# A hybrid mLSTM and gMLP step: rounding and subtraction of the state C placed ahead of each weight split, and small work of a head moved from VectorE to ScalarE

## The chip, the cores and the metric

The kernel runs on one core of one Trainium2 chip. The time is the device time of that core in microseconds. Three runs of the kernel before took 1510.98, 1510.55 and 1510.87 us, a median of 1510.87 us. All five engines run their own instruction streams and wait for each other by semaphores: TensorE (PE; PEld is its weight load), VectorE (DVE), ScalarE (ACT), GpSimd (POOL) and SyncE (SP), which issues most of the transfers.

## The reference

One layer over a prompt of 256 tokens and a batch of 8 sequences with 4 new tokens each, so 288 columns in all. Everything is fp32.

```python
h = RMSNorm_pre(x);  P = h @ w_in          # 2048 x 20496 columns: q k v o za, gates, u vb zb, ga gb
qk = silu(causal_conv4(cat(q, k)))         # depthwise, 4 taps, history from state_conv_qk
# mLSTM, 8 heads of 256, per chunk of tokens:
s    = (q . k) * wts
num  = s @ v + sc_inter * (C @ q)          # C: the old state of the head, [value x key]
den  = sum(s) + sc_inter * (n . q)
C_new = decay * C + sum ws * v k^T;  n_new = decay * n + sum ws * k
y_a = sigmoid(o) * headnorm(num / max(|den|, exp(-m))) * silu(za)
y_b = u * (tril(W_s) @ LN(vb) + b) * silu(zb)          # gMLP branch
merged = sigmoid(ga) * (y_a @ w_pa) + sigmoid(gb) * (y_b @ w_pb)
y = x + RMSNorm_post(merged @ w_out)
```

The prompt starts from a zero state. The eight sequences each have their own C and n for every head, and both are read for `C @ q` and `n . q` and written back updated.

## The kernel before, in words

**Weights.** All weights are streamed as 104 pairs of 256 columns. A pair is four chunks of 512 rows. For each chunk SyncE loads `raw[:, c]`, ScalarE rounds it to fp32r (`split_hi`, L811, `whi`), and VectorE subtracts to get the rest (`split_lo`, L1088, `wlo`). TensorE then makes 24 products of 288 columns (`chunk`, L439 to L441: hi by hi, hi by lo, lo by hi). Each of `raw`, `whi` and `wlo` has one place per chunk number, so `split_hi` of a pair's chunk c waits until TensorE has finished chunk c of the pair before. A split is therefore made nearly a whole pair ahead of its use, and each chunk on TensorE sets free the next split on ScalarE and VectorE.

**Stages.** vb pairs, u and zb pairs (gMLP), the first half of the merge, then the loop over eight heads, then the second half of the merge and the output projection. The change touches the loop over heads alone.

**A head** has five pairs on TensorE: q, k, v, o, za. The small work of the head stands between the chunks, in an order written out by hand on each engine:

- While TensorE is on the k pair, VectorE and ScalarE split the v pair. ScalarE copies q's results into a padded tile (`to_padded`, L910 and L913), VectorE makes the convolution (`conv`, L1359 and L1363; four taps by two halves of 312 columns, into `acc`, which is `hb` in the trace), and ScalarE applies Silu (L919, L921). The same is done for k one pair later.
- The old state C of sequence b is used by `inter(h, b)` on TensorE (L602 and L604, four products of about 256 columns). It stands after v chunks 1, 2, 3 (b = 0, 1, 2), o chunks 0 to 3 (b = 3 to 6) and za chunk 0 (b = 7). What it needs is made in three steps: `turn_blocks` (VectorE, L1384) transposes 32 by 32 blocks of C into `Yb`, which has two places; `ct_copy` (ScalarE, L930) rounds it to `CTh`, of which there is one, so it waits until inter(b - 1) is finished; `ct_split` (VectorE) puts n's two columns beside `CTh` (L1374) and subtracts to get `CTl` (L1375).
- After o chunk 0 TensorE makes q . k (L654), for which it needs `kv4`, a copy of k made by VectorE (L1472). After o chunk 3 it turns k and v of the sequences (L671, L672), for which it needs `ktok` from ScalarE (L972, L974) and the second part of `kv4` (VectorE, L1492). ScalarE copies these out as `kst`, `vst` and two more tiles (L978 to L982) and signals `kvs_ev`; VectorE corrects `kst` and `vst` (L1509, L1511) and signals `st_lo`.
- After za chunk 0 TensorE turns v (L685). It waits for `st_lo`, since the result goes to PSUM bank 5, from which `kst` and `vst` are read. Then come two `new_state` (L615, two products each), which need the masked values `vm` of sequence b (`of_sequence`, VectorE, L1390, four places). Six more follow by za chunk 3. VectorE adds each to the old state (`add_state`, L1397).

In the lists below a chunk's pair is the one that TensorE works on or the one that is split; the text says which.

Of the kernel before, what the change touches and what calls it, by code (L numbers as in the profile page):

```python
# [26 lines left out]
F32 = mybir.dt.float32  # L27
F32R = mybir.dt.float32r
ALU = mybir.AluOpType
# [63 lines left out]
def build(nc, x_prompt, x_sample, state_C, state_n, state_m, state_conv, g_pre, w_in, b_ig, b_fg,  # L93
# [258 lines left out]
    def of_c(b):  # L352
        return Yb[:, b % 2]
# [451 lines left out]
    def _(act):  # L805
        def split_hi(pair, c, first=False):

            act.wait_ge(raw_landed[c], 16 * pair + 16)
            if not first:
                act.wait_ge(chunk_done, 4 * pair - 3 + c)  # L810
            nc.scalar.activation(whi[:, c], raw[:, c], ACT.Copy).then_inc(hi_ready, 1)  # L811
# [106 lines left out]
        def silu(j, done):  # L918
            nc.scalar.activation(qk[:, j:j + 2, 0:TP], acc[:, :, 0:TP], ACT.Silu).then_inc(done, 1)  # L919
            for jj in range(2):  # L920
# [2 lines left out]
                    acc[:, jj, XPS:XPW].rearrange("p (b t) -> p b t", t=HIST + TS)[:, :, 0:TS],  # L923
                    ACT.Silu).then_inc(done, 1)

        def ct_copy(h, b):
            act.wait_ge(block_turned, 8 * h + b + 1)
            if b > 0:
                act.wait_ge(inter_mm, 8 * h + b)
            nc.scalar.activation(CTh[:, :, 0:DH], of_c(b), ACT.Copy).then_inc(ct_ev, 1)  # L930

        with act.Fori(0, HEADS) as h:
# [7 lines left out]
            to_padded(0, 0, q_ev)  # L940
            act.wait_ge(q_ev, 3 * h + 3)
            act.sem_inc(slot_free[0], 1)

            for c in range(CHUNKS):
                split_hi(H0 + 2 + 5 * h, c)
# [6 lines left out]
            to_padded(2, 1, k_ev)  # L952
            act.wait_ge(k_ev, 3 * h + 3)
            act.sem_inc(slot_free[1], 1)

            for c in range(CHUNKS):
                split_hi(H0 + 3 + 5 * h, c)
                ct_copy(h, c)
                if c == 2:
                    act.wait_ge(conv_step, 16 * h + 16)  # L960
                    silu(2, silu_k)
# [2 lines left out]
            act.sem_inc(slot_free[0], 1)  # L964

            for c in range(CHUNKS):
                split_hi(H0 + 4 + 5 * h, c)
                ct_copy(h, 4 + c)
                if c == 2:

                    act.wait_ge(kt_t, h + 1)
                    nc.scalar.activation(ktok[:, 0, :], ps[:, 5, 0:DH], ACT.Identity,  # L972
                                         scale=gq[:, 0, ds(h + 64, 1)])
                    nc.scalar.activation(ktok[:, 1, :], ps[:, 5, DH:2 * DH], ACT.Identity,  # L974
                                         scale=gq[:, 1, ds(h + 64, 1)]).then_inc(kt_ev, 1)
                if c == 3:
                    act.wait_ge(kvs_t, h + 1)
                    nc.scalar.activation(kst[:], ps[:, 5, 0:DH], ACT.Identity, scale=gq[:, 2, ds(h + 64, 1)])  # L978
                    nc.scalar.activation(vst[:], ps[:, 5, DH:2 * DH], ACT.Copy)
                    nc.scalar.activation(ktok[0:S, 2, :], ps[0:S, 5, 0:DH], ACT.Identity,  # L980
                                         scale=gq[0:S, 2, ds(h + 64, 1)])
                    nc.scalar.activation(vtok_h[0:S, 2, 0:DH], ps[0:S, 5, DH:2 * DH],  # L982
                                         ACT.Copy).then_inc(kvs_ev, 1)
            act.wait_ge(nn_ev, h + 1)
            nc.scalar.activation(og[:], results(1), ACT.Tanh, scale=0.5).then_inc(slot_free[1], 1)

            for c in range(CHUNKS):
                split_hi(H0 + 5 + 5 * h, c)
                if c == 0:
                    act.wait_ge(vt_t, h + 1)  # L990
                    nc.scalar.activation(vtok_h[:, 0:2, 0:DH], ps[:, 5, :].rearrange("p (t v) -> p t v", t=2),
                                         ACT.Copy).then_inc(vt_ev, 1)
                    act.wait_ge(inter_mm, 8 * h + 8)
                    nc.scalar.activation(vtok_h[S:2 * S, 2, :], ps[S:2 * S, 4, 0:DH + 2],
                                         ACT.Copy).then_inc(lo_rows, 1)
# [88 lines left out]
    def _(dve):  # L1084
# [267 lines left out]
        def conv(h, j, blk, taps):  # L1352

            for tap in taps:
                for jj in range(2):
                    w_at = par0[:, ds(2 * h + (32 * tap + blk + jj), 1)]
                    out, src = acc[:, jj, 0:CW], xp[:, j + jj, tap:tap + CW]
                    if tap == 0:
                        ins = nc.vector.tensor_scalar(out, src, w_at, par1[:, ds(2 * h + (blk + jj), 1)],  # L1359
                                                      ALU.mult, ALU.add)  # L1360
                    else:
                        dve.wait_ge(conv_step, 16 * h + (4 * j + 2 * tap + jj - 1))
                        ins = nc.vector.scalar_tensor_tensor(out, src, w_at, out, ALU.mult, ALU.add)  # L1363
                    ins.then_inc(conv_step, 1)

        def own(part_):

# [3 lines left out]
        def ct_split(h, b):  # L1371

            dve.wait_ge(ct_ev, 8 * h + b + 1)
            nc.vector.tensor_copy(CTh[:, :, DH:DH + 2], nT[:, :, ds(h + 8 * b, 1), :].squeeze(2).bitcast(F32))  # L1374
            nc.vector.tensor_tensor(CTl[:, b % 2], of_c(b), CTh[:, :, 0:DH].bitcast(F32),  # L1375
                                    ALU.subtract).then_inc(ct_lo, 1)

        def turn_blocks(h, b):
# [3 lines left out]
            if b >= 2:  # L1382
                dve.wait_ge(inter_mm, 8 * h + b - 1)
            nc.vector.transpose(of_c(b).rearrange("p k (j s) -> p j k s", s=32),  # L1384
                                Xb[:, b]).then_inc(block_turned, 1)

        def of_sequence(h, b):
            if b >= 4:
                dve.wait_ge(cs_mm, 8 * h + b - 3)
            nc.vector.tensor_scalar(vm[:, b % 4, :], vst[:].bitcast(F32), mask8[:, b:b + 1], None,  # L1390
                                    ALU.mult).then_inc(vm_set, 1)

        def add_state(h, b):
            if b % 4 == 0:
# [6 lines left out]
        with dve.Fori(0, HEADS) as h:  # L1401
# [27 lines left out]
            for c in range(CHUNKS):  # L1429
                split_lo(H0 + 2 + 5 * h, c)  # L1430
                if c == 0:
                    dve.wait_ge(q_ev, 3 * h + 3)
                    dve.wait_ge(hist_set, h + 1)
                    conv(h, 0, 0, (0, 1))
                if c == 1:
                    conv(h, 0, 0, (2, 3))
                if c == 3:
                    dve.wait_ge(silu_q, 3 * h + 3)
                    qs = Steps(dve, q_step, 2 * h)
# [5 lines left out]
                    qs(nc.vector.tensor_copy(own(0), scaled))  # L1445
                    last = nc.vector.tensor_tensor(own(S), scaled, own(0).bitcast(F32), ALU.subtract)
                    last.then_inc(qm_set, 1)
                    turn_blocks(h, 0)

            for c in range(CHUNKS):  # L1450
                split_lo(H0 + 3 + 5 * h, c)
                ct_split(h, c)
                turn_blocks(h, c + 1)
                if c == 0:
                    dve.wait_ge(k_ev, 3 * h + 3)
                    conv(h, 2, 16, (0, 1))
                if c == 1:
                    conv(h, 2, 16, (2, 3))
                if c == 2:
# [10 lines left out]
                if c == 3:  # L1470
                    dve.wait_ge(silu_k, 3 * h + 3)
                    nc.vector.tensor_copy(kv4[:, 0].rearrange("p j (n s) -> p j n s", s=S),  # L1472
                                          bc(qk[:, 2:4, TP:T], 2, [P, 2, P // S, S])).then_inc(kv4_set, 1)

                    dve.wait_ge(wsb_set, h + 1)
                    for j in range(2):
                        nc.vector.scalar_tensor_tensor(
# [6 lines left out]
                                               mybir.AxisListType.X, ALU.add))  # L1484
                    of_head = nacc[:, :, 0:NB, ds(h, 1)].squeeze(3)
                    nc.vector.tensor_tensor(of_head, of_head, added, ALU.add).then_inc(nn_ev, 1)

            for c in range(CHUNKS):
                split_lo(H0 + 4 + 5 * h, c)
                if c == 2:  # L1490
                    dve.wait_ge(v_ev, h + 1)
                    nc.vector.tensor_copy(kv4[:, 1].rearrange("p j (n s) -> p j n s", s=S),  # L1492
                                          bc(vz[:, :, TP:T], 2, [P, 2, P // S, S])).then_inc(kv4_set, 1)
                ct_split(h, 4 + c)
                if c < 3:
                    turn_blocks(h, 5 + c)
                if c == 0:
                    dve.wait_ge(s_mm, h + 1)
                    dve.wait_ge(w_exp, h + 1)
                    nc.vector.scalar_tensor_tensor(W[:, 0:384], ps[:, 5, 0:384], DH ** -0.5, W[:, 0:384],  # L1500
                                                   ALU.mult, ALU.mult)
                    nc.vector.tensor_copy(W[S:2 * S, 384:416], ident[S:2 * S, S:2 * S])
                    nc.vector.scalar_tensor_tensor(W[0:S, 384:416], ps[0:S, 5, 384:416], DH ** -0.5,
                                                   W[0:S, 384:416], ALU.mult, ALU.mult).then_inc(p_set, 1)
                if c == 3:

                    dve.wait_ge(kvs_ev, h + 1)
                    for rows in (slice(S, 2 * S), slice(3 * S, P)):
# [1 line left out]
                                                       kst[rows].bitcast(F32), ALU.mult, ALU.subtract)  # L1510
                    nc.vector.tensor_tensor(vst[2 * S:P], ps[2 * S:P, 5, DH:2 * DH], vst[2 * S:P].bitcast(F32),  # L1511
                                            ALU.subtract).then_inc(st_lo, 1)
                    dve.wait_ge(st_lo, h + 1)
                    for b in range(4):
                        of_sequence(h, b)

            for c in range(CHUNKS):
                split_lo(H0 + 5 + 5 * h, c)
                if c == 0:
                    add_state(h, 0)  # L1520
                    of_sequence(h, 4)
                    add_state(h, 1)
                    of_sequence(h, 5)
                if c == 1:

                    dve.wait_ge(num_mm, h + 1)
# [6 lines left out]
                    den(nc.vector.tensor_tensor(q3[:], q3[:], gq[:, :, ds(h + 32, 1)].squeeze(2), ALU.max))  # L1533
                    nc.vector.reciprocal(r3[:], q3[:]).then_inc(r_set, 1)
                    add_state(h, 2)
                    of_sequence(h, 6)
                    dve.wait_ge(sq_set, 3 * h + 3)
                    nc.vector.tensor_scalar(stat[:], q3[:], 1.0 / DH, EPS, ALU.mult, ALU.add).then_inc(var_set, 1)
                    add_state(h, 3)
                    of_sequence(h, 7)  # L1540
                    dve.wait_ge(rs_set, h + 1)
                    nc.vector.tensor_tensor(f3[:], r3[:], rstd[:], ALU.mult).then_inc(f_set, 1)
                if c == 2:
# [299 lines left out]
```

## Time and profile before

| | |
|---|---|
| median of three runs | 1510.87 us |
| the profiled execution | 1510.56 us |
| its span, first to last instruction | 1509.1 us |
| TensorE busy | 1486.6 us |
| VectorE busy | 935.5 us |
| ScalarE busy | 664.4 us |
| GpSimd busy | 184.5 us |
| granted TensorE clock, mean | 0.997 |
| one head, TensorE's distance from inter(0) to the next head's | about 79.1 us |

The profile is of one execution. Busy time counts an engine's instructions from start to end; on TensorE neighbours overlap, so a matmul of 288 columns lasts 0.29 us in the rows while the next starts 0.13 us after it. What matters is then the distance from one start to the next. In a row of the timeline a bracket gives the idle time before the instruction and what ended it.

### The profile page before, as it was taken

What the parts mean: (1) busy time and instruction counts of PE and PEld (TensorE: products, weight loads), DVE (VectorE), ACT (ScalarE), POOL (GpSimd) and SP (SyncE); (2) the same over time, 40 slices, a digit from 0 to 9 for tenths busy, and PEclk for the clock granted to TensorE, in tenths of its full rate; (3) what the DMA queues carried; (4) which work ended last, traced back from release to release, by engine and by line L of the source; (5) the groups of instructions that cost most, each with busy time, mean ns of one, the idle gap of its engine ahead of it and who ended that gap; (6) DMA issues with size and microseconds to landing.
All of it is one profiled execution on the core that took longest, in us unless ns stands there. A gap on an engine that the chain in (4) does not pass through costs nothing. (4 is left out here: it accounts for less than half of the span.)

```text
span 1509.1 us, 31633 instructions
## 1 busy us (share of the span) xinstructions
PE 1486.6 (99%) x11131; PEld 1472.1 (98%) x11131; DVE 935.5 (62%) x1617; ACT 664.4 (44%) x949; POOL 184.5 (12%) x331
## 2 busy tenths in 40 slices
PE   9999999999999999999999999999999999999996
PEld 9999999999999999999999999999999999999996
DVE  7756565554444458787777777786868554544444
ACT  6433433433333335454545555545455433333442
POOL 4000000001000002213030303031312000000000
PEclk9999999999999999999999999999999999999998
DMA  7765555557556577696959595959697556565543
GB/s 233 208 163 147 175 151 173 157 165 223 181 175 182 175 206 175 187 254 163 278 152 288 145 292 146 284 152 281 158 274 173 197 175 182 169 183 192 172 154 140
DMA packets 310006, 289.62 MB, mean 192 GB/s; under 512 B 82728, under 2 KB 297456, under 8 KB 309168
## 3 DMA queue, kind: packets, MB, share of 16 engines
q1 hardware_dynamic: 291424, 243.05, 57.7%
q0 software_dynamic: 18288, 45.97, 8.9%
q8 instruction: 24, 0.39, 0.1%
q14 instruction: 14, 0.11, 0.0%
q10 hardware_dynamic: 256, 0.10, 0.0%
HBM read 263.62 MB, written 25.42 MB: 192 GB/s over the span
## 5 line engine op out<-in xcount | busy, mean ns | idle before, releaser
L1088 DVE TENSOR_TENSOR wlo<-raw,whi 128x1024 fp32r<-128x1024 f32 x416 | 507.2, 1222 | 494.9 <-ACT whi L811 494.0
L439 PE MATMUL ps<-xh,whi 128*128 128x288 f32 x2560 | 760.5, 297 | 0.0
L441 PE MATMUL ps<-xh,wlo 128*128 128x288 f32 x2560 | 755.2, 295 | 0.0
L440 PE MATMUL ps<-xl,whi 128*128 128x288 f32 x2560 | 754.1, 295 | 0.0
L811 ACT ACTIVATE whi<-raw 128x1024 fp32r<-128x1024 f32 x416 | 440.5, 1060 | 711.9 <-PE ps L441 691.2
L439 PEld LDWEIGHTS ps<-xh,whi 128*128 128x128 f32 x2560 | 481.0, 188 | 0.3
L441 PEld LDWEIGHTS ps<-xh,wlo 128*128 128x128 f32 x2560 | 480.6, 188 | 0.0
L440 PEld LDWEIGHTS ps<-xl,whi 128*128 128x128 f32 x2560 | 480.3, 188 | 0.2
L440 PE MATMUL ps<-yl,whi 128*128 128x288 f32 x512 | 151.6, 296 | 0.0
L441 PE MATMUL ps<-yh,wlo 128*128 128x288 f32 x512 | 150.9, 295 | 0.0
L439 PE MATMUL ps<-yh,whi 128*128 128x288 f32 x512 | 150.1, 293 | 0.0
L439 PEld LDWEIGHTS ps<-yh,whi 128*128 128x128 f32 x512 | 96.3, 188 | 0.0
L440 PEld LDWEIGHTS ps<-yl,whi 128*128 128x128 f32 x512 | 96.2, 188 | 0.0
L441 PEld LDWEIGHTS ps<-yh,wlo 128*128 128x128 f32 x512 | 96.2, 188 | 0.0
L440 PE MATMUL ps<-ml,whi 128*128 128x288 f32 x248 | 73.4, 296 | 0.0
L439 PE MATMUL ps<-mh,whi 128*128 128x288 f32 x248 | 73.4, 296 | 0.0
L441 PE MATMUL ps<-mh,wlo 128*128 128x288 f32 x248 | 73.1, 295 | 0.0
L1769 POOL DMA_DIRECT2D out_dram<-cst x64 | 35.9, 562 | 244.4 <-DVE cst L1468 238.9
L930 ACT ACTIVATE CTh<-Yb 128x512 fp32r<-128x512 f32 x64 | 40.2, 628 | 20.3 <-PE ps L604 14.0
L439 PEld LDWEIGHTS ps<-mh,whi 128*128 128x128 f32 x248 | 46.7, 188 | 0.0
L440 PEld LDWEIGHTS ps<-ml,whi 128*128 128x128 f32 x248 | 46.6, 188 | 0.0
L441 PEld LDWEIGHTS ps<-mh,wlo 128*128 128x128 f32 x248 | 46.6, 188 | 0.0
(361 smaller groups left out, 1289.5 us busy)
## 6 DMA issues: line engine op xcount, KB each, us to landing
raw<-in_w_in_dram SPq DMA_DIRECT2D x320, 512.0 KB, 3.9
raw<-in_w_pb_dram SPq DMA_DIRECT2D x32, 512.0 KB, 3.6
Cin<-in_state_mlstm_C_dram POOLq DMA_DIRECT2D x16, 1024.0 KB, 8.7
Xb<-in_state_mlstm_C_dram SPq DMA_DIRECT2D x256, 64.0 KB, 3.8
out_dram<-Cin POOLq DMA_DIRECT2D x16, 1024.0 KB, 6.3
raw<-in_w_pa_dram SPq DMA_DIRECT2D x32, 512.0 KB, 3.5
raw<-in_w_out_dram SPq DMA_DIRECT2D x32, 512.0 KB, 3.6
part_d<-part POOLq DMA_DIRECT2D x8, 288.0 KB, 3.2
```

What stands on the lines that cost most here:

```text
L439: nc.tensor.matmul(out, whi[:, c, kk, cols], mh_[:, k, :], start=(k == 0), stop=False)
L440: nc.tensor.matmul(out, whi[:, c, kk, cols], ml_[:, k, :], start=False, stop=False)
L441: last = nc.tensor.matmul(out, wlo[:, c, kk, cols], mh_[:, k, :], start=False, stop=(k == KT - 1))
L811: nc.scalar.activation(whi[:, c], raw[:, c], ACT.Copy).then_inc(hi_ready, 1)
L930: nc.scalar.activation(CTh[:, :, 0:DH], of_c(b), ACT.Copy).then_inc(ct_ev, 1)
L1088: nc.vector.tensor_tensor(wlo[:, c], raw[:, c], whi[:, c].bitcast(F32), ALU.subtract).then_inc(lo_ready, 1)
L1769: pool.dma_start(blocks_of(conv_p_v, h, s, g), cst[g:g + 3, 2 * s:2 * s + 2, :]).then_inc(cst_out, 16)
```

## The change

Five edits, all in the loop over heads.

1. On ScalarE `ct_copy` stands ahead of `split_hi` in each step of the k-side and v-side loops; on VectorE `ct_split` and the next `turn_blocks` stand ahead of `split_lo`. Before, each split came first.
2. n's two columns of `CTh` are written by ScalarE in `ct_copy` and no longer by VectorE in `ct_split`.
3. The first tap of the convolution (`first_tap`) is an Identity activation with scale and bias on ScalarE, right after q's and k's results are copied.
4. The masked values `vm` (`of_sequence`) are made by ScalarE: four after `og`'s Tanh and ahead of the next split, two and two after the splits of chunks 1 and 2.
5. On VectorE `turn_blocks` of b = 0 and 1 both stand after the v pair's split 2. The sums for n (L1477 to L1486) move from the end of one loop to after the za pair's split 1, and the products of `W` (`p_set`) and the second `kv4` come after `ct_split`, `turn_blocks` and `split_lo` of their step.

```diff
+        def first_tap(h, j, blk):
+            for jj in range(2):
+                nc.scalar.activation(acc[:, jj, 0:CW], xp[:, j + jj, 0:CW], ACT.Identity,
+                                     bias=par1[:, ds(2 * h + (blk + jj), 1)],
+                                     scale=par0[:, ds(2 * h + (blk + jj), 1)]).then_inc(conv_step, 1)
+
+        def of_sequence(h, b):
+            if b >= 4:
+                act.wait_ge(cs_mm, 8 * h + b - 3)
+            nc.scalar.activation(vm[:, b % 4, :], vst[:].bitcast(F32), ACT.Identity,
+                                 scale=mask8[:, b:b + 1]).then_inc(vm_set, 1)
+
         def ct_copy(h, b):
             act.wait_ge(block_turned, 8 * h + b + 1)
             if b > 0:
                 act.wait_ge(inter_mm, 8 * h + b)
+            nc.scalar.activation(CTh[:, :, DH:DH + 2], nT[:, :, ds(h + 8 * b, 1), :].squeeze(2).bitcast(F32), ACT.Copy)
             nc.scalar.activation(CTh[:, :, 0:DH], of_c(b), ACT.Copy).then_inc(ct_ev, 1)
...
             act.sem_inc(slot_free[0], 1)
+            act.wait_ge(hist_set, h + 1)
+            first_tap(h, 0, 0)
...
-
-            for c in range(CHUNKS):
+            first_tap(h, 2, 16)
+
+            for c in range(CHUNKS):
+                ct_copy(h, c)
                 split_hi(H0 + 3 + 5 * h, c)
-                ct_copy(h, c)
...
             for c in range(CHUNKS):
+                ct_copy(h, 4 + c)
                 split_hi(H0 + 4 + 5 * h, c)
-                ct_copy(h, 4 + c)
...
             nc.scalar.activation(og[:], results(1), ACT.Tanh, scale=0.5).then_inc(slot_free[1], 1)
+            act.wait_ge(st_lo, h + 1)
+            for b in range(4):
+                of_sequence(h, b)
 
             for c in range(CHUNKS):
                 split_hi(H0 + 5 + 5 * h, c)
+                if c == 1:
+                    of_sequence(h, 4)
+                    of_sequence(h, 5)
+                if c == 2:
+                    of_sequence(h, 6)
+                    of_sequence(h, 7)
...
             dve.wait_ge(ct_ev, 8 * h + b + 1)
-            nc.vector.tensor_copy(CTh[:, :, DH:DH + 2], nT[:, :, ds(h + 8 * b, 1), :].squeeze(2).bitcast(F32))
...
-                    conv(h, 0, 0, (0, 1))
+                    conv(h, 0, 0, (1,))
                 if c == 1:
                     conv(h, 0, 0, (2, 3))
+                if c == 2:
+                    turn_blocks(h, 0)
+                    turn_blocks(h, 1)
...
-                    turn_blocks(h, 0)
-
-            for c in range(CHUNKS):
+
+            for c in range(CHUNKS):
+                ct_split(h, c)
+                if c > 0:
+                    turn_blocks(h, c + 1)
                 split_lo(H0 + 3 + 5 * h, c)
-                ct_split(h, c)
-                turn_blocks(h, c + 1)
                 if c == 0:
                     dve.wait_ge(k_ev, 3 * h + 3)
-                    conv(h, 2, 16, (0, 1))
+                    conv(h, 2, 16, (1,))
...
+            for c in range(CHUNKS):
+                ct_split(h, 4 + c)
+                if c < 3:
+                    turn_blocks(h, 5 + c)
+                split_lo(H0 + 4 + 5 * h, c)
+                if c == 2:
+                    dve.wait_ge(v_ev, h + 1)
+                    nc.vector.tensor_copy(kv4[:, 1].rearrange("p j (n s) -> p j n s", s=S),
+                                          bc(vz[:, :, TP:T], 2, [P, 2, P // S, S])).then_inc(kv4_set, 1)
```

**Where ScalarE's order moves.** The engine is ScalarE, at the end of the steps that split the za pair, when TensorE has finished o chunk 3. `whi<-raw` is `split_hi` of za chunk 3, `CTh<-Yb` is `ct_copy` of b = 7, `kst`, `vst`, `ktok`, `vtok_h` are the copies that end in `kvs_ev`, and `og` is the Tanh. Before:

```order
L811 ACTIVATE whi<-raw 128x1024 [waits chunk_done,raw_landed3]
L927 REGISTER_ALU
L930 ACTIVATE CTh<-Yb 128x2x256 [waits inter_mm,block_turned]
L978 ISA [waits kvs_t]
L978 ACTIVATE kst<-ps,gq 128x256
L979 ACTIVATE vst<-ps 128x256
L980 ACTIVATE ktok<-ps,gq 32x256
L982 ACTIVATE vtok_h<-ps 32x256
L985 ACTIVATE og<-ps 128x576 [waits nn_ev]
```

After:

```order
L939 REGISTER_ALU
L942 ISA [waits inter_mm,block_turned]
L942 ACTIVATE CTh<-nT 128x2x2
L943 ACTIVATE CTh<-Yb 128x2x256
L811 ACTIVATE whi<-raw 128x1024 [waits chunk_done,raw_landed3]
L994 ISA [waits kvs_t]
L994 ACTIVATE kst<-ps,gq 128x256
L995 ACTIVATE vst<-ps 128x256
L996 ACTIVATE ktok<-ps,gq 32x256
L998 ACTIVATE vtok_h<-ps 32x256
L1001 ACTIVATE og<-ps 128x576 [waits nn_ev]
L935 ACTIVATE vm<-vst,mask_56 128x256 [waits st_lo]
```

The copy of C now stands ahead of the split, and both still stand ahead of `kst`; the split now lies between the wait for `inter_mm` and `kst`. Behind `og` there is a wait for `st_lo` and four copies to `vm`.

**Where VectorE's order moves, I.** The engine is VectorE, one step earlier (split of za chunk 2, TensorE on o chunk 3). `kv_134<-vz` is the second part of `kv4`, for which TensorE's L671 waits; `CTl` is `ct_split`, `Yb<-Xb` is `turn_blocks`. Before:

```order
L1087 REGISTER_ALU
L1088 TENSOR_TENSOR wlo<-raw,whi 128x1024 [waits hi_ready]
L1492 COPY kv_134<-vz 128x256 [waits v_ev]
L1373 REGISTER_ALU
L1374 ISA [waits ct_ev]
L1374 COPY CTh<-nT 128x2x2
L1375 TENSOR_TENSOR CTl<-Yb,CTh 128x512
L1384 STREAM_TRANSPOSE Yb<-Xb 128x8x2x32 [waits inter_mm]
```

After:

```order
L1393 REGISTER_ALU
L1394 TENSOR_TENSOR CTl<-Yb,CTh 128x512 [waits ct_ev]
L1403 STREAM_TRANSPOSE Yb<-Xb 128x8x2x32 [waits inter_mm]
L1112 REGISTER_ALU
L1113 TENSOR_TENSOR wlo<-raw,whi 128x1024 [waits hi_ready]
L1498 COPY kv_134<-vz 128x256 [waits v_ev]
```

The copy to `kv4` stood behind the split alone; now `ct_split` (with its wait for `ct_ev`) and `turn_blocks` stand ahead of the split too.

**Where VectorE's order moves, II.** The engine is VectorE, at the start of the steps that split the o pair (TensorE on v chunks 1 and 2). `qm` is the last work on q. Before:

```order
L1446 TENSOR_TENSOR qm<-qp,qm 128x2x8x4 [waits q_step]
L1381 REGISTER_ALU
L1384 STREAM_TRANSPOSE Yb<-Xb 128x8x2x32 [waits block_in0]
L1087 ISA
L1088 TENSOR_TENSOR wlo<-raw,whi 128x1024 [waits hi_ready]
L1373 ISA
L1374 REGISTER_ALU [waits ct_ev]
L1374 COPY CTh<-nT 128x2x2
L1375 TENSOR_TENSOR CTl<-Yb,CTh 128x512
L1384 STREAM_TRANSPOSE Yb<-Xb 128x8x2x32
L1359 ISA [waits k_ev]
```

After:

```order
L1462 TENSOR_TENSOR qm<-qp,qm 128x2x8x4 [waits q_step]
L1393 ISA
L1394 TENSOR_TENSOR CTl<-Yb,CTh 128x512 [waits ct_ev]
L1112 ISA
L1113 TENSOR_TENSOR wlo<-raw,whi 128x1024 [waits hi_ready]
L1383 REGISTER_ALU [waits k_ev]
L1384 ISA [waits conv_step]
L1384 SCALAR_TENSOR_TENSOR hb<-xp,par_58,hb 128x312
```

The transposition of b = 0 is gone from this place (it stands a step earlier), `ct_split` of b = 0 stands ahead of the split, the transposition of b = 1 is gone too, and of the convolution only the second tap is left here.

## Rows read from the trace of the kernel before

**Rows 1.** The page: busy time of each engine.

```profile
PE 1486.6 (99%) x11131; PEld 1472.1 (98%) x11131; DVE 935.5 (62%) x1617; ACT 664.4 (44%) x949; POOL 184.5 (12%) x331
```

**Rows 2.** Who waited for whom, TensorE weight loads: us in total, times, longest.

```profile
PEld ps L602 <- DVE CTl L1375: 12.7, 24, 1.1
...
PEld ps L685 <- issue: 2.3, 8, 0.3
...
PEld ps L654 <- DVE kv L1472: 1.9, 8, 0.2
```

**Rows 3.** Timeline of TensorE, third head: start us, us, what, count.

```profile
741.75 0.29 PE L441 MATMUL ps<-xh,wlo 128*128 128x288 f32 x1
...
742.97 0.28 PE L604 MATMUL ps<-CTl,qm 128*128 128x256 f32 x1
...
743.09 0.29 PE L439 MATMUL ps<-xh,whi 128*128 128x288 f32 x1
...
754.66 0.48 PE L654 MATMUL ps<-qk 128*128 128x256 f32 x1
```

**Rows 4.** Timeline of VectorE, third head, the same stretch.

```profile
739.96 0.70 DVE L1384 STREAM_TRANSPOSE Yb<-Xb 128x512 f32<-128x512 f32 x1
...
740.59 1.19 DVE L1088 TENSOR_TENSOR wlo<-raw,whi 128x1024 fp32r<-128x1024 f32 x1
...
741.76 0.68 DVE L1375 TENSOR_TENSOR CTl<-Yb,CTh 128x512 fp32r<-128x512 f32 x1
...
742.37 0.70 DVE L1384 STREAM_TRANSPOSE Yb<-Xb 128x512 f32<-128x512 f32 x1
...
744.57 1.22 DVE L1088 TENSOR_TENSOR wlo<-raw,whi 128x1024 fp32r<-128x1024 f32 x1
...
754.36 0.25 DVE L1472 COPY kv<-qk 128x256 f32<-128x256 f32 x1
```

**Rows 5.** Timeline of ScalarE, third head, the same stretch.

```profile
737.21 0.28 ACT L913 ACTIVATE xp<-ps 128x32 f32<-128x32 f32 x2
...
738.89 1.06 ACT L811 ACTIVATE whi<-raw 128x1024 fp32r<-128x1024 f32 x1 [1.40 <-PE ps L441]
...
743.34 0.63 ACT L930 ACTIVATE CTh<-Yb 128x512 fp32r<-128x512 f32 x1 [0.20 <-PE ps L604]
```

**Rows 6.** Third head, last chunk of the o pair: timelines of TensorE, then VectorE.

```profile
764.77 0.29 PE L439 MATMUL ps<-xh,whi 128*128 128x288 f32 x1
...
767.96 0.27 PE L671 MATMUL ps<-ident,kv 128*128 128x128 f32 x1
...
765.15 1.23 DVE L1088 TENSOR_TENSOR wlo<-raw,whi 128x1024 fp32r<-128x1024 f32 x1 [1.15 <-ACT whi L811]
...
766.29 0.29 DVE L1492 COPY kv<-vz 128x256 f32<-128x256 f32 x1
```

**Rows 7.** Third head, last o chunk to new states: ScalarE, VectorE, TensorE.

```profile
768.22 1.06 ACT L811 ACTIVATE whi<-raw 128x1024 fp32r<-128x1024 f32 x1 [1.82 <-PE ps L441]
...
769.19 0.62 ACT L930 ACTIVATE CTh<-Yb 128x512 fp32r<-128x512 f32 x1
...
769.71 0.46 ACT L978 ACTIVATE kst<-ps,gq 128x256 fp32r<-128x256 f32 x1
...
770.06 0.37 ACT L979 ACTIVATE vst<-ps 128x256 fp32r<-128x256 f32 x1
...
771.25 0.99 DVE L1509 SCALAR_TENSOR_TENSOR kst<-ps,gq,kst 32x256 fp32r<-32x256 f32 x2
...
772.71 1.15 DVE L1390 TENSOR_SCALAR vm<-vst,mask 128x256 fp32r<-128x256 f32 x4
...
768.75 0.29 PE L604 MATMUL ps<-CTl,qm 128*128 128x256 f32 x1
...
772.82 0.63 PE L685 MATMUL ps<-ident,vz 128*128 128x128 f32 x4
...
773.21 0.72 PE L615 MATMUL ps<-kst,vm 128*128 128x256 f32 x4
```

More of the change, by code:

```diff
@@ L1357, in conv @@
                     out, src = acc[:, jj, 0:CW], xp[:, j + jj, tap:tap + CW]
[L1358 to L1364, printed above, removed]
+                    dve.wait_ge(conv_step, 16 * h + (4 * j + 2 * tap + jj - 1))
+                    nc.vector.scalar_tensor_tensor(out, src, w_at, out, ALU.mult, ALU.add).then_inc(conv_step, 1)
         def own(part_):
@@ L1385, in turn_blocks @@
                                 Xb[:, b]).then_inc(block_turned, 1)
[L1387 to L1391, printed above, removed]
         def add_state(h, b):
@@ L1473, in _ @@
                                           bc(qk[:, 2:4, TP:T], 2, [P, 2, P // S, S])).then_inc(kv4_set, 1)
+            for c in range(CHUNKS):
[7 more added lines that the diff above has]
+                                          bc(vz[:, :, TP:T], 2, [P, 2, P // S, S])).then_inc(kv4_set, 1)
+                if c == 0:
+                    dve.wait_ge(s_mm, h + 1)
+                    dve.wait_ge(w_exp, h + 1)
+                    nc.vector.scalar_tensor_tensor(W[:, 0:384], ps[:, 5, 0:384], DH ** -0.5, W[:, 0:384],
+                                                   ALU.mult, ALU.mult)
+                    nc.vector.tensor_copy(W[S:2 * S, 384:416], ident[S:2 * S, S:2 * S])
+                    nc.vector.scalar_tensor_tensor(W[0:S, 384:416], ps[0:S, 5, 384:416], DH ** -0.5,
+                                                   W[0:S, 384:416], ALU.mult, ALU.mult).then_inc(p_set, 1)
+                if c == 1:
                     dve.wait_ge(wsb_set, h + 1)
@@ L1486, in _ @@
                     nc.vector.tensor_tensor(of_head, of_head, added, ALU.add).then_inc(nn_ev, 1)
-            for c in range(CHUNKS):
[L1489 to L1504, printed above, removed]
                 if c == 3:
@@ L1512, in _ @@
                                             ALU.subtract).then_inc(st_lo, 1)
-                    dve.wait_ge(st_lo, h + 1)
-                    for b in range(4):
-                        of_sequence(h, b)
             for c in range(CHUNKS):
@@ L1520, in _ @@
                     add_state(h, 0)
-                    of_sequence(h, 4)
                     add_state(h, 1)
-                    of_sequence(h, 5)
                 if c == 1:
@@ L1535, in _ @@
                     add_state(h, 2)
-                    of_sequence(h, 6)
                     dve.wait_ge(sq_set, 3 * h + 3)
@@ L1539, in _ @@
                     add_state(h, 3)
-                    of_sequence(h, 7)
                     dve.wait_ge(rs_set, h + 1)
```

## The prediction

> **What bounds the kernel now.** The page comes first: TensorE is busy for 1486.6 us, 99% of the span, so only what TensorE waits for can move the time [rows 1]. VectorE and ScalarE have room as a share; relief there is worth something only at a place where TensorE waits. So the waits come second. In the loop over heads TensorE's weight loads wait at three places: for `CTl` ahead of inter(b), 24 times in 8 heads, so three times in each; for `kv` ahead of the q . k products (L654), once in each; and 0.3 us ahead of L685, put down to "issue" [rows 2]. L685 waits for `st_lo`, and a chain below shows that this is what it meets. Third comes the timeline of one undisturbed head, the third, engine by engine at these places. There a chunk takes 767.96 - 764.77 = 3.19 us, or 0.133 a product [rows 6], and inter(b) four times 0.12 = 0.48 us (742.97 to 743.09 is one) [rows 3].
>
> **Part A: from v chunk 1 to q . k (L654).** Before, VectorE does turn 0 (739.96), the split (740.59), `CTl` (741.76), and TensorE, which could begin inter(0) at 741.75 + 0.13 = 741.88, ends it at 743.09, where 741.88 + 0.48 = 742.36 was possible [rows 3, 4]. The change takes turn 0 from here, puts it in VectorE's idle time two steps earlier, and puts `CTl` ahead of the split: VectorE is free for it at 739.96. Its input comes from ScalarE, which ends q's sibling copies (k's) at 737.49 and then waits 1.40 us for TensorE [rows 5]. In this gap go two first taps (312 columns; between 0.35 for 256 columns, 769.71 to 770.06 [rows 7], and 0.63 for 512 [rows 5]), n's columns and the copy of 0.63: done by about 739.6, so the taps and the small copy cost nothing here. `CTl` takes 0.61 (741.76 to 742.37) and is there at 740.6. Inter(0) no longer waits.
>
> Next, ct_copy(1) must wait until inter(0) is finished: last product 0.16 into the next chunk (742.97 + 0.28 = 743.25 against 743.09), and ScalarE starts 0.09 later [rows 3, 5]. So 742.36 + 0.16 + 0.09 = 742.61. n's columns on ScalarE are not in the trace; I bound them by 0.06 or less from below (VectorE's form hardly moves its neighbour, and nothing excludes less) and 0.20 from above, and take 0.14, half of the 0.28 of two copies of 32 columns [rows 5]. With the copy's 0.63 and 0.05 for the semaphore, `CTl`(1) starts at 743.43. From there to `kv` VectorE has the same work as before from the split at 744.57 to `kv` at 754.36, 9.79 us with no idle time in between [rows 4], only in another order. Three small casts drop out (about 0.1) and about as much is lost waiting for ct_copy(3). So `kv` starts at about 743.43 + 9.79 = 753.22 and ends 0.25 later, and L654, at 754.66 before [rows 3], starts at 753.5. TensorE would be ready at 742.36 + 2 x 0.48 + 3 x 3.19 = 752.9, so it waits some 0.6 us for `kv` where all earlier waits were. **A gives back 1.16 us a head**, between 0.9 and the full 1.8.
>
> The Trainium skill ("VectorE: DVE Perf Modes", section on the TRN2 errata) speaks against moving such small work: it gives ScalarE a fixed 224 cycles of 1.2 GHz for each instruction from SBUF, paid anew by each small one, so 0.19 us for n's two columns. The trace has 0.28 for two small copies from PSUM, overlapped [rows 5]. By the page's figure A, B and C below would each be 0.05 us worse, 1.2 us in all over eight heads.
>
> **Part B: o chunk 3 to L671.** L671 needs the second `kv`. Before, it stood right behind the split: start 766.29, end 766.58, with L671 at 767.96 and 1.4 us to spare [rows 6]. Now `CTl`(6) and turn 7 stand ahead of that split, and `CTl`(6) hangs on inter(5), which ends as chunk 3 starts. From that start: 0.16 + 0.09 + 0.14 + 0.63 + 0.05 = 1.07 until `CTl`; 0.61 for it, 0.63 for the turn (739.96 to 740.59 [rows 4]), 1.14 for the split (765.15 to 766.29 [rows 6]), 0.29 for `kv` and 0.05: 3.79 us against the chunk's 3.19. `ktok`, the other thing L671 waits for, follows that copy on ScalarE: 0.25 + 0.14 + 0.52 + 0.97 for copies and split (part C has the rows) + 0.35 + 0.46 = 2.7 us, in time. **B is a new wait of 0.6 us a head**, between 0.3 and 0.8.
>
> **Part C: `st_lo` and L685.** Before, ScalarE splits at 768.22, copies C at 769.19 and starts `kst` at 769.71; VectorE's correction runs from 771.25 to 772.71, and TensorE's L685 starts at 772.82 [rows 7]. That is 3.11 us from `kst` to L685 in one unbroken chain, though chunk and inter(7) are done before: L671 767.96, inter(6) done and the chunk begun 0.13 after 768.75, so 768.88 + 3.19 + 0.48 = 772.55. The wait of 0.27 us matches the 2.3 us of eight heads called "issue". Now ScalarE may not split first: it waits for inter(6) to be finished (768.75 + 0.29 = 769.04), then 0.09, n's columns 0.14, the copy 0.52 (769.19 to 769.71) and the split 0.97 (768.22 to 769.19). `kst` starts at 770.76 where it was 769.71 [rows 7]. Before, ScalarE used the 0.8 us in which TensorE made the transpositions and inter(6) for the split; now it idles there. Nothing covers this, since L685 already waited. **C is 1.05 us a head**, between 0.9 and 1.3. Queued behind L685 are both new states and za chunk 1.
>
> **Part D: `vm`.** VectorE made it from 772.71 on; TensorE asks for the first at 773.21 and the second 0.28 later [rows 7]. The ScalarE form, from SBUF with a scale, is not in the trace: between 0.37 (plain, 256 columns) and 0.46 (with a scale), each 0.35 after the other, by the two rows from PSUM. I take 0.46. Started at 772.78, the first is there at 773.29, 0.08 late, the second at 773.64, 0.07 later still: **0.15 us a head**, 0 to 0.35. Behind `vm` on ScalarE stand the next pair's split and v's copy for the products after za chunk 1. After `st_lo` they need 0.07 + 4 x 0.35 + 0.97 + two copies of at most 0.63 = 3.7 us; TensorE asks for them after 0.11 (772.71 to 772.82) + 0.39 + 0.15 + 0.56 of products + 3.19 = 4.4 us: cost nothing, with 0.7 us to spare. The other four `vm` fall into steps with a whole chunk before their use, as do the sums for n. VectorE's relief (eight `vm`, casts, four taps) is worth nothing beyond A, as no later wait of TensorE is on it.
>
> **Sum.** -1.16 + 0.60 + 1.05 + 0.15 = +0.64 us a head, times eight +5.1 us. Against the profiled execution, 1510.56 us (span 1509.1), that is 1515.7; the median of the runs is 0.3 above that execution, so 1516.0.
>
> **Rivals.**
> - *Only A counts (faster).* The copy and subtraction come early enough and B and C stay where they were. For it: three of the five waits per head are on `CTl`, the largest sum in rows 2, and VectorE loses 1.15 us of `vm` in one piece [rows 7]. Against it: `kst` stands behind both the copy and the split in ScalarE's order. It would give 8 x 1.16 = 9.3 us back: 1501.6. It decides where `kst` starts no more than 0.1 us later after L671 than now. Chance 0.10.
> - *A draw.* `kv` is in time for L654, so A gives the full 1.8, or B is hidden: -1.8 + 0.6 + 1.05 + 0.15 = 0, or -1.16 + 0 + 1.2 = 0.04: about 1511. For it: A's wait for `kv` and B are both small differences of long chains. Against it: A's chain has no idle time that could shrink. Chance 0.20.
> - *ScalarE falls behind (slower than forecast).* If `first_tap`, `vm` and n's columns cost their upper bounds and do not overlap, A, B and C are 0.06 worse each and D 0.2, and v's copy after `vm` eats up the 0.7 us to spare ahead of the products after za chunk 1 and is some 0.3 late: together 0.7 us more a head, 1521.6. Chance 0.12.
>
> My forecast has 0.58. Of these, a difference within 0.2% (3 us) can't be told from none. Faster by more than that: 0.10 and the tail of the draw, 0.11 in all. Same: 0.20. Slower: 0.69. The range of 8 in 10 reaches from 1509, most of the draw, to 1522, the last rival.
>
> **What would show it.** In the profile after: no wait of the `CTh` products for `CTl`; a wait of about 0.6 us at q . k for `kv`; a wait of about 0.6 us at the transpositions of k and v (none before) whose releaser is the second `kv`; the gap ahead of L685 grown from 0.27 to about 1.3 us; small waits for `vm`. L671 to L685 should be 5.9 us, where it is 4.86. The prediction is wrong if that distance stays under 5.3, or if the L671 transpositions follow o chunk 3 with no gap.

## The result and the profile after

| | before | after |
|---|---|---|
| median of 6 runs each | 1510.78 us | 1516.95 us |
| lowest to highest | 1510.35 to 1511.14 | 1516.74 to 1517.25 |
| span of the profiled execution | 1509.1 us | 1515.2 us |

The ratio is 1.0041, with a 95% interval of 1.0029 to 1.0052: slower by 6.2 us, where 5.1 us were forecast. Of all the runs in this document one fell in a slow state, at 2823.51 us (the masked values back on VectorE); without it the median of that kernel is 1515.0 us and not 1515.09. The page of the changed kernel answers to [rows 1]; its columns are busy us, share of the span and count, by engine:

```profile
PE 1484.1 (98%) x11131; PEld 1472.2 (97%) x11131; DVE 904.0 (60%) x1457; ACT 707.5 (47%) x1109; POOL 183.8 (12%) x331
```

VectorE has lost 31.5 us of work (935.5 to 904.0) and ScalarE has gained 43.1 us (664.4 to 707.5). Neither number says anything about the time. What does is the list of TensorE's waits (us in all, times, longest). [rows 2] has the waits of the weight loads (PEld); the matmuls (PE) wait a little less for the same events, and their list names what L685 waits for. Both are shown for L685:

```profile
PE ps L685 <- DVE vst L1527: 9.4, 8, 1.2
...
PE ps L654 <- DVE kv L1488: 3.6, 8, 0.5
...
PE ps L671 <- DVE kv L1498: 3.6, 8, 0.5
...
PEld ps L685 <- issue: 10.8, 8, 1.4
```

As weight loads L654 and L671 wait 5.5 us each, so against [rows 2] L685's wait went from 2.3 to 10.8 us, L654's from 1.9 to 5.5, L671's from nothing to 5.5, and L602's from 12.7 to nothing. There are three waits in each head, and none is on `CTl` any more. Two are on the copies to `kv` and one is on `vst`, the last step ahead of `st_lo`. Now the third head on TensorE (start, duration, instruction, idle time before it and what ended it), where [rows 3, 6, 7] were taken before; the last line is of the kernel before, the end of step D there:

```profile
742.94 0.30 PE L441 MATMUL ps<-xh,wlo 128*128 128x288 f32 x1
...
743.08 0.28 PE L602 MATMUL ps<-CTh,qm 128*128 128x258 f32 x1
...
743.44 0.29 PE L604 MATMUL ps<-CTl,qm 128*128 128x256 f32 x1
...
753.96 0.29 PE L441 MATMUL ps<-xh,wlo 128*128 128x288 f32 x1
...
754.71 0.92 PE L654 MATMUL ps<-qk 128*128 128x256 f32 x3 [0.45 <-DVE kv L1488]
...
764.81 0.29 PE L439 MATMUL ps<-xh,whi 128*128 128x288 f32 x1
...
768.61 0.33 PE L671 MATMUL ps<-ident,kv 128*128 128x128 f32 x1 [0.45 <-DVE kv L1498]
...
769.46 0.29 PE L604 MATMUL ps<-CTl,qm 128*128 128x256 f32 x1
...
774.58 0.63 PE L685 MATMUL ps<-ident,vz 128*128 128x128 f32 x4 [1.18 <-DVE vst L1527]
...
775.13 0.83 PE L615 MATMUL ps<-kst,vm 128*128 128x256 f32 x4
...
775.80 0.29 PE L439 MATMUL ps<-xh,whi 128*128 128x288 f32 x1
...
773.77 0.30 PE L439 MATMUL ps<-xh,whi 128*128 128x288 f32 x1
```

Read it by distances from start to start, which don't depend on where the head begins:

| step, third head | before | after | change | forecast |
|---|---|---|---|---|
| A: last product of v chunk 1 to L654 | 12.91 | 11.77 | -1.14 | -1.16 |
| B: L654 to L671 | 13.30 | 13.90 | +0.60 | +0.60 |
| C: L671 to L685 | 4.86 | 5.97 | +1.11 | +1.05 |
| D: L685 to za chunk 1 (after: 775.80; before: 773.77) | 0.95 | 1.22 | +0.27 | +0.15 |

VectorE in the same head shows the chains behind it:

```profile
741.16 0.68 DVE L1394 TENSOR_TENSOR CTl<-Yb,CTh 128x512 fp32r<-128x512 f32 x1
...
744.68 0.69 DVE L1394 TENSOR_TENSOR CTl<-Yb,CTh 128x512 fp32r<-128x512 f32 x1 [0.80 <-ACT CTh L943]
...
754.37 0.28 DVE L1488 COPY kv<-qk 128x256 f32<-128x256 f32 x1
...
765.93 0.69 DVE L1394 TENSOR_TENSOR CTl<-Yb,CTh 128x512 fp32r<-128x512 f32 x1 [0.29 <-ACT CTh L943]
...
767.17 1.18 DVE L1113 TENSOR_TENSOR wlo<-raw,whi 128x1024 fp32r<-128x1024 f32 x1
...
768.27 0.28 DVE L1498 COPY kv<-vz 128x256 f32<-128x256 f32 x1
...
773.01 0.98 DVE L1525 SCALAR_TENSOR_TENSOR kst<-ps,gq,kst 32x256 fp32r<-32x256 f32 x2
...
774.01 0.43 DVE L1527 TENSOR_TENSOR vst<-ps,vst 64x256 fp32r<-64x256 f32 x1
```

`CTl`(0) starts at 741.16, with TensorE's inter(0) at 743.08: in time, as forecast. `CTl`(1) starts at 744.68, and from there to `kv` (754.37) are 9.69 us without idle time, the 9.79 of [rows 4] in another order. Ahead of `CTl`(1) VectorE is idle for 0.80 us, which matters for the first tap below. Then the B chain: `CTl`(6), turn 7, split and `kv`, from 765.93 to 768.27 + 0.28, in one piece, and L671 starts at 768.61. The correction of `kst` and `vst` begins at 773.01. On ScalarE, the chain ahead of it:

```profile
743.92 0.21 ACT L942 ACTIVATE CTh<-nT 128x4 fp32r x1 [2.25 <-PE ps L604]
...
744.03 0.62 ACT L943 ACTIVATE CTh<-Yb 128x512 fp32r<-128x512 f32 x1
...
769.95 0.21 ACT L942 ACTIVATE CTh<-nT 128x4 fp32r x1 [2.38 <-PE ps L604]
...
770.06 0.62 ACT L943 ACTIVATE CTh<-Yb 128x512 fp32r<-128x512 f32 x1
...
770.58 1.04 ACT L811 ACTIVATE whi<-raw 128x1024 fp32r<-128x1024 f32 x1
...
771.53 0.46 ACT L994 ACTIVATE kst<-ps,gq 128x256 fp32r<-128x256 f32 x1
...
774.47 1.71 ACT L935 ACTIVATE vm<-vst,mask 128x256 fp32r<-128x256 f32 x4 [1.08 <-DVE vst L1527]
```

The copy of C cannot begin before inter(6) is over (769.46 + 0.29 = 769.75 on TensorE). The copy, then the split, then `kst` at 771.53 follow each other, 2.92 us after L671 where it was 1.75 before [rows 6, 7].

### The profile page after: what moved, and what is told of

The parts are those of the page before. It is cut to its first block and busy times, and to the rows that moved or that the text cites. A ratio compares the mean times of both kernels' runs of the same rounds, so it can differ in the third digit from the quotient of the medians.

```text
span 1515.2 us, 31641 instructions
## 1 busy us (share of the span) xinstructions
PE 1484.1 (98%) x11131; PEld 1472.2 (97%) x11131; DVE 904.0 (60%) x1457; ACT 707.5 (47%) x1109; POOL 183.8 (12%) x331
## 5 line engine op out<-in xcount | busy, mean ns | idle before, releaser
L1394 DVE TENSOR_TENSOR CTl<-Yb,CTh 128x512 fp32r<-128x512 f32 x64 | 44.2, 691 | 57.0 <-ACT CTh L943 56.8
L942 ACT ACTIVATE CTh<-nT 128x4 fp32r x64 | 13.1, 205 | 129.1 <-PE ps L604 129.1
```

What stands on the lines that cost most here:

```text
L942: nc.scalar.activation(CTh[:, :, DH:DH + 2], nT[:, :, ds(h + 8 * b, 1), :].squeeze(2).bitcast(F32), ACT.Copy)
```

## The experiments

Two theories. **Order**: each reordering gives or costs what its own chain says, and work moved between the engines costs only where it lies in such a chain. **Load**: ScalarE was given too much (taps, n's columns, masked values), and that is where the time went. All times are medians; the kernel before was run beside each group, at 1510.4 to 1510.6 us. That is 0.2 to 0.3 us less than the 1510.78 beside the changed kernel, and the changed kernel was not run again: "came back" means the distance to its 1516.95 us, and can be off by as much.

### C undone on ScalarE (1513.24 us)

```diff
-                ct_copy(h, 4 + c)
-                split_hi(H0 + 4 + 5 * h, c)
+                if c == 3:
+                    split_hi(H0 + 4 + 5 * h, c)
+                    ct_copy(h, 4 + c)
+                else:
+                    ct_copy(h, 4 + c)
+                    split_hi(H0 + 4 + 5 * h, c)
```

> The changed kernel, with ScalarE's old order in one step only: at za chunk 3 the split stands ahead of the copy of C again. Order theory (each edit of the order costs or gives what its own chain says): kst starts 1.06 us earlier after L671, L685's wait falls from 1.33 to about 0.3 us in each head, 8 x 1.06 = 8.5 us less, 1508.5. Rival, load theory (the time is lost because ScalarE now carries the taps, n's columns and the masked values): 0 to 2 us less, 1515 to 1517.

Only 3.7 us came back, where 8.5 were expected, though more than the load theory allows. ScalarE did its part: L671 starts at 767.67, so `kst` is 1.97 us after it, 0.95 earlier than in the changed kernel. The first line is the end of inter(6) on TensorE:

```profile
768.53 0.28 PE L604 MATMUL ps<-CTl,qm 128*128 128x256 f32 x1
...
767.32 1.06 ACT L811 ACTIVATE whi<-raw 128x1024 fp32r<-128x1024 f32 x1 [0.69 <-PE ps L441]
...
769.01 0.21 ACT L942 ACTIVATE CTh<-nT 128x4 fp32r x1 [0.62 <-PE ps L604]
...
769.64 0.46 ACT L998 ACTIVATE kst<-ps,gq 128x256 fp32r<-128x256 f32 x1
...
770.62 0.36 ACT L1002 ACTIVATE vtok_h<-ps 32x256 f32<-32x256 f32 x1
```

But VectorE did not follow:

```profile
769.77 0.69 DVE L1398 TENSOR_TENSOR CTl<-Yb,CTh 128x512 fp32r<-128x512 f32 x1 [2.15 <-ACT CTh L943]
...
770.38 1.22 DVE L1117 TENSOR_TENSOR wlo<-raw,whi 128x1024 fp32r<-128x1024 f32 x1
...
771.62 0.99 DVE L1529 SCALAR_TENSOR_TENSOR kst<-ps,gq,kst 32x256 fp32r<-32x256 f32 x2
```

`vtok_h`, the last copy that `kvs_ev` signals, was over at 770.98, and the correction began only at 771.62, right behind VectorE's own split (770.38). That split stands behind `CTl`(7), which waits for ScalarE's copy. So VectorE's half of the same edit makes a second chain, hidden as long as both are there: in the changed kernel ScalarE's last copy (`vtok_h`, 772.51 + 0.36) ends at 772.87 and VectorE's split (771.66 + 1.23) at 772.89. L685 starts 5.53 us after L671:

```profile
767.67 0.33 PE L671 MATMUL ps<-ident,kv 128*128 128x128 f32 x1 [0.45 <-DVE kv L1502]
...
773.20 0.63 PE L685 MATMUL ps<-ident,vz 128*128 128x128 f32 x4 [0.73 <-DVE vst L1531]
```

### C undone on both engines (1509.21 us)

The edit above on ScalarE, and on VectorE:

```diff
             for c in range(CHUNKS):
+                if c == 3:
+                    split_lo(H0 + 4 + 5 * h, c)
                 ct_split(h, 4 + c)
                 if c < 3:
                     turn_blocks(h, 5 + c)
-                split_lo(H0 + 4 + 5 * h, c)
+                    split_lo(H0 + 4 + 5 * h, c)
```

> The changed kernel with the old order at za chunk 3 on both engines: the split ahead of the copy of C on ScalarE, the split ahead of the subtraction of C on VectorE. In the run with ScalarE's half alone VectorE started the correction of kst at 3.95 us after L671, behind its split, where it was 3.29 before. Theory: C has two chains, one on each engine, and undoing one leaves the other; with both undone L685's wait falls to 0.3 to 0.4 us and the time to about 1509.3. Rival: the rest of the wait is ScalarE's (kst is 0.1 us later, more copies in its row): no more than 0.5 us below ScalarE's half alone, 1513.

It came out at 1509.21, 7.7 us below the changed kernel. TensorE's waits:

```profile
PE ps L654 <- DVE kv L1492: 3.6, 8, 0.5
...
PE ps L671 <- DVE kv L1504: 3.6, 8, 0.5
...
PE ps L685 <- DVE vst L1533: 1.9, 8, 0.2
```

L685's wait fell from 9.4 to 1.9 us, and the other two are untouched. In the third head L685 starts 5.03 us after L671 (766.61 to 771.64), where it was 5.97 in the changed kernel and 4.86 before. So nearly all of C is shown, with two chains and not one; the last 0.17 us a head did not go with the order. It is about what n's copy, which is still on ScalarE here, costs that engine's chain (0.21 us, shown below).

### B undone: the second kv copy early (1511.78 us)

```diff
             for c in range(CHUNKS):
+                if c == 2:
+                    dve.wait_ge(v_ev, h + 1)
+                    nc.vector.tensor_copy(kv4[:, 1].rearrange("p j (n s) -> p j n s", s=S),
+                                          bc(vz[:, :, TP:T], 2, [P, 2, P // S, S])).then_inc(kv4_set, 1)
                 ct_split(h, 4 + c)
...
-                if c == 2:
-                    dve.wait_ge(v_ev, h + 1)
-                    nc.vector.tensor_copy(kv4[:, 1].rearrange("p j (n s) -> p j n s", s=S),
-                                          bc(vz[:, :, TP:T], 2, [P, 2, P // S, S])).then_inc(kv4_set, 1)
```

The copy now stands at the head of its step, ahead of the split too, where it did not stand in the kernel before.

> The changed kernel, with VectorE's second kv copy ahead of the subtraction of C and the turn in its step. Order theory: the wait of 0.6 us ahead of L671 goes in every head and nothing takes its place, since the st_lo chain is counted from L671: 4.9 us less, 1512.1. Load theory: no change. A third outcome, that the wait reappears at L671 for ktok (ready about 0.5 us before the chunk ends) or at L685: under 2 us less.

5.2 us came back, and of the three waits two are left, unchanged to 0.1 us:

```profile
PE ps L685 <- DVE vst L1527: 9.4, 8, 1.2
...
PE ps L654 <- DVE kv L1488: 3.6, 8, 0.5
```

### What was left of A: the first kv copy early (1511.09 us)

The same edit for `kv4[:, 0]`, ahead of `ct_split` of b = 3.

> The changed kernel, with VectorE's first kv copy ahead of the subtraction of C for b = 3. Order theory: the 0.6 us wait ahead of L654 goes, 4.9 us less, 1512.0; this would show that the rest of the wait for CTl had only moved to kv. Load theory: no change.

5.9 us came back, 1.0 more than expected. So this wait was the remainder of A: without it part A, with the first tap and the earlier transpositions in it, gives back about 1.9 us a head (1.14 + 5.9 / 8), where the prediction had 1.8 for its full worth. Both early copies gave more than the 0.6 us a head of the chain, 0.65 and 0.73.

### The masked values back on VectorE (1515.09 us)

`of_sequence` as it was before, on VectorE, in its old places.

> The changed kernel, with the masked values vm made by VectorE again. Order theory: only the 0.27 us a head between L685 and za chunk 1 goes, 2.2 us less, 1514.8, and L685's wait stays 1.33. Load theory: most of the loss of 6.2 us goes, 1511 to 1512.

1.9 us came back, near the order theory's 2.2; the load theory wanted 5 or 6. L685's wait stayed at 9.4 us.

### The masked values on ScalarE in the kernel before (1512.44 us)

The same edit the other way round, by itself.

> The kernel before with one edit: the masked values vm on ScalarE, in the same places as in the changed kernel. Order theory: 0.27 us a head between L685 and za chunk 1, 2.2 us more than before, 1513.0. Load theory: most of the 6.2 us, 1515 to 1517.

2.0 us more than the 1510.48 beside it (ratio 1.0014, 1.0004 to 1.0023). The edit costs the same from either side, and the waits of TensorE's weight loads are those of [rows 2], also at L685 (2.3 us) and L654 (1.9 us):

```profile
PEld ps L602 <- DVE CTl L1390: 12.7, 24, 1.0
```

### The first tap on ScalarE in the kernel before (1505.43 us)

`first_tap` of the change, by itself, and `conv` without tap 0.

> The kernel before with one edit: the convolution's first tap on ScalarE. Order theory: VectorE has 0.67 us less between the subtractions for b = 0 and 1, the waits for CTl(1) and CTl(2) go, CTl(0)'s stays, L654 starts 0.67 us earlier in each head: 5.3 us less than before, 1505.5. Load theory: 0 to 3 us more than before.

5.1 us less than the 1510.48 beside it (0.9967, 0.9955 to 0.9980); the order theory said 5.3. More work on ScalarE made the kernel faster, which the load theory can't explain. VectorE was without a gap at this place, so its taps lay in A's chain; the line is of the kernel before:

```profile
742.99 0.75 DVE L1359 TENSOR_SCALAR hb<-xp,par,par 128x312 f32<-128x312 f32 x2
```

The waits of the weight loads in the run, against 12.7, 1.9 and 2.3 us:

```profile
PEld ps L602 <- DVE CTl L1379: 7.2, 16, 1.0
...
PEld ps L654 <- DVE kv L1476: 2.5, 8, 0.3
...
PEld ps L685 <- issue: 2.3, 8, 0.3
```

24 waits for `CTl` have become 16, where 8 were expected: the one for `CTl`(1) went, the one for `CTl`(2) shrank from 0.53 to 0.17 us in the third head. L685 waits as before and L654 0.6 us more in all, so the time came out right and one wait did not.

### n's columns back on VectorE (1515.96 us)

```diff
-            nc.scalar.activation(CTh[:, :, DH:DH + 2], nT[:, :, ds(h + 8 * b, 1), :].squeeze(2).bitcast(F32), ACT.Copy)
...
+            nc.vector.tensor_copy(CTh[:, :, DH:DH + 2], nT[:, :, ds(h + 8 * b, 1), :].squeeze(2).bitcast(F32))
```

> The changed kernel with n's two columns written by VectorE again, right ahead of its subtraction. On ScalarE they delay the copy by 0.11 us, on VectorE they delayed the subtraction by 0.06, and three stretches per head hang on this: 8 x 3 x 0.05 = 1.2 us less, 1515.7. Load theory (small work is what costs ScalarE the time): 3 us less or more.

1.0 us came back, where 1.2 were expected. It did not come as expected, 0.05 us at each of three places. As matmul waits, L685's fell from 9.4 to 8.0 us, L654's rose from 3.6 to 3.9 and L671's stayed at 3.6. The run also shows what the copy of n's columns costs ScalarE. These are inter(0)'s end and the copy of C behind it:

```profile
743.16 0.29 PE L604 MATMUL ps<-CTl,qm 128*128 128x256 f32 x1
...
743.54 0.63 ACT L942 ACTIVATE CTh<-Yb 128x512 fp32r<-128x512 f32 x1 [2.25 <-PE ps L604]
```

The copy of C starts 0.09 us after the matmul's end (743.45). In the changed kernel it starts 0.30 us after it (743.73 to 744.03), with n's columns in between: they cost ScalarE's chain 0.21 us, and back on VectorE they are not free there either.

### All four, five, and the best order (1499.97, 1496.12 and 1493.22 us)

First the split first on ScalarE, both kv copies early and vm on VectorE, together:

> The changed kernel with the four edits of the first series together: split ahead of the copy of C at za chunk 3, both kv copies early, vm on VectorE. Order theory: the four add up, 8 x (1.06 + 0.6 + 0.6 + 0.27) = 20.2 us less than the changed kernel, 1496.7. Load theory: no better than the best of them alone.

17.0 us less than the changed kernel. One by one the four gave 3.7 + 5.2 + 5.9 + 1.9 = 16.7: they add up. The 20.2 us expected had the C edit at its full 8.5. The only wait left in a head:

```profile
PE ps L685 <- DVE vst L1522: 5.9, 8, 0.7
```

With VectorE's split first at za chunk 3 as well:

> The four edits together with VectorE's old order at za chunk 3 as well. Theory of two chains: 0.5 to 0.6 us a head less than the four, 1495 to 1496. Rival: 1500, as the four.

1496.12 us, 3.9 below the four (0.48 a head, where the two chains said 0.5 to 0.6). Last, a new order for that step. On ScalarE the split goes behind `kst`, `vst` and the two other copies; `vst` is signalled by itself (TensorE waits for the second signal as well), and VectorE's correction and `vm` stand ahead of its split. The second `kv` copy stays early. Of the diff this is ScalarE's order:

```diff
                 ct_copy(h, 4 + c)
-                split_hi(H0 + 4 + 5 * h, c)
+                if c < 3:
+                    split_hi(H0 + 4 + 5 * h, c)
...
+            split_hi(H0 + 4 + 5 * h, 3)
             act.wait_ge(nn_ev, h + 1)
```

> As the four together, but at za chunk 3 ScalarE makes the copy of C first, then kst and vst (signalled by themselves) and the two other tiles, and splits last; VectorE corrects kst and vst ahead of its split. Order theory: st_lo comes 4.2 us after L671 where TensorE asks at 4.6, so the last 0.3 us wait at L685 goes as well: 2 to 3 us below the four together, 1494. Rival: the split of za chunk 3, now last, makes TensorE wait at za chunk 3: not below the four.

1493.22 us, 6.7 below the four together, where 2 to 3 were expected, and 1.15% below the kernel before (ratio 0.9885, 0.9869 to 0.9902). The list of TensorE's waits has none in the loop over heads any more; what is left lies at the start and the end of the kernel, 1.8 us at the most:

```profile
PE ps L455 <- POOL ident L1669: 1.8, 1, 1.8
```

## Why the prediction was right

**Sign and size.** +0.64 us a head was forecast. The four steps of the third head sum to +0.84, or 6.7 us in eight heads, and 6.2 were measured. Some 0.4 us of the difference lies in the second head of the kernel before, where inter(0) waited 0.84 us for `CTl` and not 0.46 as in the others; that wait went too:

```profile
663.38 0.39 PE L602 MATMUL ps<-CTh,qm 128*128 128x258 f32 x1 [0.84 <-DVE CTl L1375]
```

So the 1.1 us between forecast and result are D's 1.0, C's 0.5 and A's 0.2 us in eight heads, less these 0.4; the last 0.2 us are not traced. That A and B came out to 0.02 us a head is in part luck: their terms were off by up to 0.1 us in both directions and cancelled.

**A** came out as worked out, the wait for `kv` included (0.62 us of extra distance between the last product and L654; forecast 0.6). `CTl`(1) started 1.60 us after the start of inter(0) (743.08 to 744.68), where the forecast had 1.55, and VectorE's stretch was 9.69 us, not 9.79: the idle time that was expected ahead of `CTl`(3) did not come. That L654 was held by that copy and by nothing else is shown by the run with it early.

**B** came out at 3.80 us from the chunk's start to L671 (764.81 to 768.61; forecast 3.79): `CTl`(6) started at 1.12 and not 1.07, and the steps behind it took 2.68 us and not 2.72. **C** was 0.06 too small. `kst` came 1.17 us later after L671 (1.75 to 2.92), not 1.05. The small copy delays the next by 0.11 us (769.95 to 770.06, forecast 0.14), but it starts 0.20 after inter(6) is over, where 0.09 was read in [rows 3, 5]. This comes with n's copy and not with the order: in the run with the split first on ScalarE, the old order with n's copy, it is 0.20 as well (768.81 to 769.01), and in the run with the columns back on VectorE, the new order without it, 0.09. Its address is computed in registers, which may be the reason; that is not shown. From `kst` to L685 it was then 3.05 us where [rows 7] had 3.11.

C had a second chain, on VectorE, that the prediction did not name. It did not change the sum, since both end at the same time, but it would have led to the wrong repair: 8.5 us were expected from ScalarE's half alone and 3.7 came. The trace of the kernel before had shown it already. The 3.11 us were called one unbroken chain behind `kst`, but in these rows VectorE's subtraction of C ends last, at 771.21, ScalarE's copies at 771.04, and the correction starts at 771.25:

```profile
770.53 0.68 DVE L1375 TENSOR_TENSOR CTl<-Yb,CTh 128x512 fp32r<-128x512 f32 x1
...
770.68 0.36 ACT L982 ACTIVATE vtok_h<-ps 32x256 f32<-32x256 f32 x1
```

**D** was the term that was mis-sized, 0.27 for 0.15. A `vm` on ScalarE took 0.50 us and the next started 0.40 after it (1.71 for four), where the prediction had taken 0.46 and 0.35 from a copy with a scale out of PSUM, whose source differs. And L615 starts 0.16 us after the first `vm` is over (774.97 to 775.13), where the prediction had 0.05 for a semaphore at every step; no row was given for the 0.05. From either side the runs give 1.9 and 2.0 us in eight heads.

**The small copies.** The trace has 0.205 us for one copy of n's columns (the mean of 64), and it costs ScalarE's chain 0.21 us, where the sum had 0.14. `CTl`(1) and `CTl`(6) came 0.05 us later than forecast. The section on the TRN2 errata in "VectorE: DVE Perf Modes" of the Trainium skill gives 0.19 with its 224 cycles. The trace agrees, and by the page's figure the total would have been 6.3 us against 5.1. 6.2 were measured, and the two come near each other in part by chance: the largest part of the difference is D's, and with the columns back on VectorE the 1.0 us came back at L685 and not in equal parts at A, B and C.

**The rivals.** That A alone counts fell because `kst` started 1.17 us later after L671, not 0.1. The draw needed `kv` in time for L654 or L671, and it was late at both. ScalarE did not fall behind: v's copy after `vm` caused no wait. The prediction's statement that VectorE's relief is worth nothing beyond A was not tested by a run of its own. In the kernel before the first tap alone is worth 5.1 us, because it lies in A's chain. In the changed kernel VectorE is idle for 0.80 us ahead of `CTl`(1), more than the 0.67 us of the tap's two halves (742.99 to 743.66 before): the reordering and the tap seem to give back the same microseconds, and the tap is then worth nothing there. This is read from the trace; no run takes the tap out of the changed kernel.

## What to carry to other kernels

Moving a step ahead of another in a list helps the chain that it heads and delays everything behind it by what it now waits for: a copy that waits for a late matmul, put ahead of work that was ready, turns its engine's busy time into idle time. So count each reordering from the event that the moved step waits for to the next thing that the busy engine asks of this list, one place at a time; here it was worth -1.1 us a head at one place of the loop (with the first tap moved as well) and +0.6 and +1.1 at two others. Where undoing it on one engine gives back less than the sum says, look for the same edit on the engine behind it.

## What the runs showed of the hardware

- A ScalarE Identity from SBUF with a scale for each partition took 0.50 us for 256 columns, and the next started 0.40 after it (1.71 for four). A plain copy of 512 columns from SBUF took 0.62, and 256 from PSUM 0.37 (plain) and 0.46 (with a scale). So a row with the same number of columns is the right neighbour only if its source and its operands are the same too.
- The copy of n's four columns took 0.205 us on ScalarE, and from a matmul's end to the copy of C behind it there were 0.30 us with it and 0.09 without.
- A matmul that follows a wait costs a little beyond the wait: L671 after it has 0.16 us to the next transposition (768.61 to 768.77 in the changed kernel), where 0.11 is usual, and L602 has 0.23 to L604 (742.50 to 742.73 in the kernel before), where it has 0.12 without a wait (743.08 to 743.20 in the changed kernel).
